# A two-layer diffusion block on one core: layer 0's context tiles part at the query projection, tile 2 goes alone to its first expert choice

## The reference, cut to what matters

```python
# layer 0: pooling mixer and grouped attention side by side; layer 1: windowed attention with sinks
h = rmsnorm(x) * (1 + scale) + shift            # shift, scale, gate: SiLU(c) @ ada_w, per layer and stream
u, q, k, v = split(h @ w_in)                    # layer 0: q and k get an RMSNorm per head
y = concat(pool(u), attention(q, k, v)) @ w_out # a context query sees context keys only
x = x + gate * y
# PEER, per tile of 128 tokens, 8 heads
q  = h2 @ w_q                                   # 1024 x 2048: 256 columns a head
s1, s2 = q[..., :128] @ keys1.T, q[..., 128:] @ keys2.T
# top 16 of s1 and of s2 -> 256 pairs -> top 16 pairs: idx, softmax g
a = gelu(u_tab[idx] . h2)                       # 16 rows of 1024 per token and head, gathered
x = x + gate2 * sum(g * a * v_tab[idx])         # 16 more rows of 1024
```

## Time and profile before

| | |
|---|---|
| runs | 2435.02, 2441.13, 2445.78 us |
| span of the profiled execution | 2436.4 us |
| time of the profiled execution beyond its span | none is given |
| busy | PE 1404.1, DVE 1540.4, POOL 1493.3, ACT 353.7 us |
| moved by DMA | 936.93 MB, 385 GB/s over the span |
| chain that ended last | DMA 35%, POOL 22%, PE 21%, DVE 10%, issue 9% |

### The profile page before, as it was taken

The page is one execution under the profiler, slowest core; times in us unless marked ns, Lnnn a source line. Parts: engine busy times, 40 slices in busy tenths (PEclk is TensorE's granted clock), DMA queues, the critical chain, the costliest instruction groups (busy, mean ns, idle before and its releaser), DMA issues.

```text
span 2436.4 us, 22069 instructions
## 1 busy us (share of the span) xinstructions
PE 1404.1 (58%) x7150; PEld 637.7 (26%) x7150; DVE 1540.4 (63%) x4020; ACT 353.7 (15%) x740; POOL 1493.3 (61%) x1546
## 2 busy tenths in 40 slices
PE   7998863456676574345434446458856555434334
PEld 2456420123323251011001113125623133100000
DVE  1339768878945756767776556412799646777543
ACT  1321210122301011011001002112123011000000
POOL 0005677677676766777777677520477775777772
PEclk9999986677787786677567757678988767566556
DMA  9957999999999999999999999996999999999997
GB/s 346 352 188 287 378 406 408 409 409 409 381 405 409 406 407 407 409 409 409 409 409 409 405 409 409 403 337 239 338 408 400 403 408 406 409 409 409 410 410 305
DMA packets 286802, 936.93 MB, mean 385 GB/s; under 512 B 27729, under 2 KB 28513, under 8 KB 286433
## 3 DMA queue, kind: packets, MB, share of 16 engines
q0 software_dynamic: 221184, 805.40, 83.4%
q1 hardware_dynamic: 65504, 130.12, 14.5%
HBM read 934.36 MB, written 1.05 MB: 384 GB/s over the span
## 4 chain that ended last, share of the span: by engine, by line
DMA 35%; POOL 22%; PE 21%; DVE 10%; issue 9%; ACT 2%; SPq 1%; DVEq 0%; POOLq 0%; ACTq 0%
DMA RING<-in_p_v,IDV 19%; POOL RING L868 15%; DMA RING<-in_p_u,IDX 5%; PE acc L1508 5%; PE wk L1762 5%; DVE RING L949 3%; PE wk L1745 3%; PE wk L1586 3%; POOL WR L868 2%; DMA BC<-in_p_v,IDV 2%; DMA X<-in_p_v,IDV 2%; POOL BC L868 1%; DMA RING<-in_o_w_in 1%; POOL H L868 1%; PE wk L1539 1%
## 5 line engine op out<-in xcount | busy, mean ns | idle before, releaser
L949 DVE SCALAR_TENSOR_TENSOR RING<-RING,acc 128x1024 f32<-128x1024 f32 x576 | 687.6, 1219 | 292.9 <-DMA RING<-in_p_u,IDX 272.8
L1508 PE MATMUL acc<-RING,ST 128*32 128x512 f32 x2020 | 531.5, 914 | 521.4 <-DMA RING<-in_p_v,IDV 463.8
L868 POOL DMA_INDIRECT RING<-in_p_u,IDX x576 | 561.7, 975 | 420.7 <-DVE IDX L1257 193.3
L868 POOL DMA_INDIRECT RING<-in_p_v,IDV x505 | 490.7, 972 | 224.5 <-issue 142.0
L1508 PEld LDWEIGHTS acc<-RING,ST 128*32 128x32 f32 x2020 | 99.7, 144 | 750.4 <-issue 743.4
L1508 PE MATMUL acc<-WR,ST 128*32 128x512 f32 x428 | 160.5, 945 | 65.5 <-DMA BC<-in_p_v,IDV 56.1
L1508 PE MATMUL acc<-X,ST 128*32 128x512 f32 x304 | 124.1, 943 | 104.8 <-DMA RING<-in_p_v,IDV 104.8
L868 POOL DMA_INDIRECT H<-in_p_u,IDX x82 | 78.2, 953 | 126.9 <-DVE IDX L1257 99.2
L949 DVE SCALAR_TENSOR_TENSOR H<-H,acc 128x1024 f32<-128x1024 f32 x82 | 100.0, 1220 | 81.4 <-DMA H<-in_p_u,IDX 80.1
L868 POOL DMA_INDIRECT WR<-in_p_v,IDV x107 | 101.1, 945 | 41.7 <-issue 31.1
L1508 PE MATMUL acc<-BC,ST 128*32 128x512 f32 x156 | 79.3, 947 | 72.4 <-DMA X<-in_p_v,IDV 58.2
(11 more groups left out here) (258 smaller groups left out, 2405.3 us busy)
## 6 DMA issues: line engine op xcount, KB each, us to landing
RING<-in_ada_w SPq DMA_DIRECT2D x25, 1024.0 KB, 14.2
WR<-in_ada_w SPq DMA_DIRECT2D x21, 1024.0 KB, 13.2
WR<-in_p_w_q SPq DMA_DIRECT2D x20, 1024.0 KB, 13.0
RING<-in_p_u,IDX POOLq DMA_INDIRECT x576, 17.6
WR<-in_e_w_in SPq DMA_DIRECT2D x8, 1024.0 KB, 11.7
RING<-in_p_v,IDV POOLq DMA_INDIRECT x505, 18.4
...
```

Source lines behind the costliest of these rows:

```text
L868: pool.indirect_dma_start(out=row_at(row), out_offset=None, in_=tables[kind], in_offset=bass.IndirectOffsetOnAxis(ap=rows, axis=0)).then_i ...
L949: nc.vector.scalar_tensor_tensor(out=row_at(row), in0=row_at(row), scalar=1.0, in1=acc[:, 1, :], op0=ALU.mult, op1=ALU.mult, accum_out=A[: ...
L1508: ins = nc.tensor.matmul(acc[32 * g:32 * g + 32, 0, hf * 512:hf * 512 + 512], ST[:, c % 2, s, :], row_at(rows[g][0])[:, hf * 512:hf * 512 ...
```

## The change

Layer 0's front and its steps 0 to 7 are written anew:
- `("in", 0, 1)` (most of q) is cut into tile 2 and tile 3, on the same kept blocks. Tile 2's q norm stands between them; tile 3's, and its transpose, inside the attention.
- `("ada", 1, 0, 2)` (4 blocks) moves from ahead of the attention to behind `out`; `("ada", 0, 10, 2)` (4 blocks) moves behind the score of head 1; `("ada", 1, 2, 1)` (2 blocks) moves to step 4, `("ada", 1, 3, 1)` from step 4 to 5.
- `out`, `normA`, `normB`, `hT` and `score` of heads 0 and 1 run for tile 2 alone. A score of one tile alone has a new form: tokens stand still and 256 weight columns pass (8 products), the result is turned by two transposes ("T") and multiplied with the keys (2 products); before, weights stood still and each head took 16 products.
- Tile 3's `out` moves to step 0, its norm to steps 1 and 2, its heads 0 and 1 to step 3, on kept blocks. The scores of both tiles move: heads 2 and 3 from ahead of step 0 to step 2, heads 4 and 5 from 0 to 4, heads 6 and 7 from 3 to 5.
- The choice for heads 2 and 3 starts at step 3 instead of 1, later ones by about one step.
- `block_slots` loses its fixed round: each block takes the allowed slot that is idle longest.
- `BC` row 0 is no longer lent to the first `u` gathers, and `H` row 0 to `v` from step 4 instead of 0.
- The ten small loads are issued by ACT's queue instead of SP's.
- Switches `ALONE` and `HEAD_FIRST` go; layer 1 keeps its order, but its scores take the new form.

```diff
-    s += [("in", 0, 1, ctx), ("adaT", 0, 6, 2), ("adaD", 0, 6, 2)]
-    s += [("poolB", CTX, 0), ("poolB", CTX, 1), ("poolB", CTX, 2), ("poolB", CTX, 3)]
-    s += [("rope", 0, t, "q", p) for t in ctx for p in range(2)]
-    s += [("ada", 1, 0, 2), ("adaT", 1, 0, 2), ("adaD", 1, 0, 2)]
-    s += [("tqk", 0, 2, "q"), ("tqk", 0, 3, "q")]
...
+    s += [("in", 0, 1, (2,)), ("rope", 0, 2, "q", 0), ("rope", 0, 2, "q", 1), ("in", 0, 1, (3,)), ("adaT", 0, 6, 2), ("adaD", 0, 6, 2)]
+    s += [("poolB", CTX, g) for g in range(4)]
+    s += [("tqk", 0, 2, "q")]
+    s += att_close(0, CTX, 0, 12, {0: [("rope", 0, 3, "q", 0)], 1: [("rope", 0, 3, "q", 1), ("ada", 0, 8, 2)], 2: [("tqk", 0, 3, "q")],
+                                   3: [("adaT", 0, 8, 2)], 4: [("adaD", 0, 8, 2)], 5: [("bc", 0, CTX, G1)]})
+    s += [("out", 0, (2,), 0), ("outD", 0, (2,), 0), ("out", 0, (2,), 1), ("ada", 1, 0, 2), ("outD", 0, (2,), 1), ("normA", 0, 2, 2), ("normB", 0, 2, 2),
+          ("adaT", 1, 0, 2), ("hT", 0, 2, (2,)), ("adaD", 1, 0, 2)]
+    s += [("score", 0, (2,), (0,)), ("xin", 0, 2), *[("topk", 0, 2, (0,), p) for p in range(3)]]
+    s += [("score", 0, (2,), (1,)), ("ada", 0, 10, 2), ("topk", 0, 2, (1,), 0), ("topk", 0, 2, (1,), 1)]
+    return s + [("adaT", 0, 10, 2), ("adaD", 0, 10, 2)]
...
+    put(f, 0, ("out", 0, (3,), 0), ("outD", 0, (3,), 0), ("out", 0, (3,), 1))
+    next_choices(f, 0, 2, (3, 4, 5, 6, 7))
+    put(f, 1, ("outD", 0, (3,), 1), ("normA", 0, 2, 3))
+    put(f, 2, ("normB", 0, 2, 3), ("hT", 0, 2, (3,)), ("score", 0, ctx, (2, 3)))
+    put(f, 3, ("score", 0, (3,), (0, 1)))
+    put(f, 4, ("score", 0, ctx, (4, 5)))
+    put(f, 4, ("ada", 1, 2, 1), ("adaT", 1, 2, 1), ("adaD", 1, 2, 1))
+    put(f, 5, ("score", 0, ctx, (6, 7)))
+    put(f, 5, ("ada", 1, 3, 1))
...
-    choose(f, 0, 2, (6, 7), (12, 13, 14, 15, 16))
+    choose(f, 0, 2, (6, 7), (13, 14, 15, 16, 17))
...
-EXTRA = [(("bc", 0), "u", 0, 5), (("bc", 1), "u", 0, 5), (("bc", 2), "u", 0, 5), (("h", 0), "v", 0, 22),
+EXTRA = [(("bc", 1), "u", 0, 5), (("bc", 2), "u", 0, 5), (("h", 0), "v", 4, 22),
...
-                sp.dma_start(KR[:, 2 * l, :], t["p_keys1"][l]).then_inc(loaded["keys"], 16)
+                act.dma_start(KR[:, 2 * l, :], t["p_keys1"][l]).then_inc(loaded["keys"], 16)
```

More of the change, by code:

```diff
@@ new lines, in fills1 @@
+    put(f, 0, ("score", 1, first, (4, 5)))
+    put(f, 1, ("score", 1, first, (6, 7)), ("in", 1, 0, second), ("in", 1, 1, second))
+    put(f, 1, ("adaD", 1, 10, 2))
+    put(f, 4, ("rope", 1, 1, "q", 1), ("rope", 1, 1, "q", 2))
+    put(f, 5, ("tqk", 1, 1, "q"))
+    choose(f, 1, 0, (4, 5), (8, 9, 10, 11, 12))
+    att_wide(f, 1, LAT, 5, 8, 16)
+    choose(f, 1, 0, (6, 7), (14, 15, 16, 17, 18))
+    out_blocks(f, 1, second, 17)
+    put(f, 21, ("normA", 1, 2, 1))
+    put(f, 22, ("normB", 1, 2, 1))
@@ L317, in fills1 @@
+    put(f, 23, ("hT", 1, 2, second))
+    for heads, n in zip(((6, 7), (0, 1), (2, 3), (4, 5)), (24, 25, 27, 29)):
+        put(f, n, ("score", 1, second, heads))
+    choose(f, 1, 1, (0, 1), (26, 27, 28, 29, 30))
+    choose(f, 1, 1, (2, 3), (33, 34, 35, 36, 37))
+    choose(f, 1, 1, (4, 5), (40, 41, 42, 43, 44))
+    choose(f, 1, 1, (6, 7), (45, 46, 47, 48, 49))
     put(f, 52, ("normA", 1, 3, 0))
@@ L430, in block_slots @@
 def block_slots():
-    early = next(i for i, name in enumerate(BLOCKS) if name[0] == "score")
     end = AT["ada", 1, 4, 2]
@@ L437, in block_slots @@
     dots = [AT["experts", l, ORDER[l][0], 0, 0] for l in range(DEPTH)]
-    slots, users, idle = [], {}, {s: (-1, s) for s in (*range(WSLOTS), XSLOT)}
+    slots, users, idle = [], {}, {s: (-1, s) for s in range(XSLOT + 1)}
     idle.update({s: (AT["experts_end", 0], s) for s in RSLOTS})
@@ L1350, in _ @@
                     elif (c, tiles[0]) == (2, 0):
-                        for a in range(3):
+                        for a in range(1 - l, 3):
                             act.wait_ge(*emptied(("bc", a), 49 * l))
@@ L1754, in _ @@
                     w = [weights(s + (jh,)) for jh in range(2)]
+                    for h in heads if len(tiles) == 1 else ():
+                        o = begin(s + ("Q", h))
+                        for j in range(KC):
+                            if h == heads[0] and j % 4 == 0:
+                                pe.wait_ge(*evac(tokens + (j // 4,)))
+                            ins = nc.tensor.matmul(o[:, 0:2 * P], HTS[tiles[0] // 2][:, j, tiles[0] % 2 * P:tiles[0] % 2 * P + P],
+                                                   w[j // 4][:, j % 4, h % 2 * 2 * P:(h % 2 + 1) * 2 * P], start=(j == 0), stop=(j == KC - 1))
+                        done(ins)
+                    for h in heads if len(tiles) == 1 else ():
+                        pe.wait_ge(*evac(s + ("Q", h)))
+                        o = begin(s + ("T", h))
+                        for half in range(2):
+                            ins = tr(o[:, half * P:half * P + P], QS[:, h % 2, 0, half * P:half * P + P])
+                        done(ins)
+                    for h in heads if len(tiles) == 1 else ():
+                        pe.wait_ge(*evac(s + ("T", h)))
+                        o = begin(s + ("R", h))
+                        for half in range(2):
+                            ins = nc.tensor.matmul(o[:, half * P:half * P + P], QS[:, h % 2, 1, half * P:half * P + P], KT[:, 2 * l + half, :],
+                                                   start=True, stop=True)
+                        done(ins)
+                    if len(tiles) == 1:
+                        continue
                     for h in heads:
```

219 lines of the change are left out of this document (71 added, 148 removed).

## The result

The changed kernel took 2493.34 us (four runs, 2486.21 to 2494.24), the kernel before, run beside it, 2443.45: 1.0205 of it, 95% interval 1.0184 to 1.0226. The forecast was +26 us on the median and the time is +50, 2.3 us past the upper end of the stated range (2491); the profiled span went from 2436.4 to 2484.4, +48.0. The direction was right, the size half.

A forecast was written before the change was run, and what follows sets the result against it. Gathers were taken as bound by bytes at 409 GB/s, the front as starving the DMA. A 53rd gather 28.6 us later, less 3.2 for bytes, plus 1.1 for layer 1 gave +26: 2441.1 to 2467 us, range 2425 to 2491.

The forecast's parts named there:

- Small loads: Start of the front: with ACT issuing the ten loads, SP's weight blocks start earlier, -4.4 us (bounds 0 and -4.4).
- Query projection: Front, ahead of `out`: split by tile, with tile 2's norm under tile 3's part, -7.2 us (bounds 0 and -11.9).
- `out` to hT: Front, tile 2 alone: from the start of `out` to hT 21.1 us instead of 35.5, -14.4 us.
- hT to IDX: Front, first score and choice: 18.2 us instead of 22.3, -4.1 us (bounds -2 and -5), IDX written at 165.3.
- Step 1: DVE behind the first IDX: tile 3's `out` from 172.8 to 179.8, its norm ready at 199, TensorE waiting from 187.
- Steps 2 and 3: Score of heads 2 and 3 done at 218, tile 3's products end at 229.7; `v` 2 waits until then, DMA idles 30 us.
- Steps 4 to 6: First `v` sums from 237.7, `ada` 1 2 landing at 265.5, DVE waiting until 269, heads 6 and 7 until 290.5, latent hT 307.
- Step 7: POOL's 53rd gather, into H row 3, at 307 instead of 278.43: 28.6 us later, less 3.2 us for bytes moved, 25.4.
- Clock: TensorE after waits of 10 us: slower products, four such gaps up to 6.5 us, left to the range; time then 2473.
- Layer 1: Layer 1's lone-tile scores: a transpose and a copy added ahead of its first choice, +1.1 us (bounds 0 and +4).
- the faster one: Rival, chance 0.16: the early IDX carries through, 53rd gather before about 253, gain 9.5 to 19 us, middle 2427.
- The much slower one: Rival, chance 0.11: POOL stops a third time, row sums of head 1 behind `in` 2 and its blocks, 2490 us.

The follow-up runs named there:

- e1: The kernel before with only the ten small loads issued by ACT's queue: 0.9986 of the kernel before.
- e9: The changed kernel run again, unaltered: 1.0212 of the kernel before.
- e14: The kernel before with heads 4 and 5 scored at step 4 instead of 0, heads 6 and 7 at 5 instead of 3: 1.0141 of the kernel before.
- e18: The same kernel as e14, run again on another chip: 1.0134 of the kernel before.
- e10: The changed kernel with scores of heads 4 to 7 at step 3 and `ada` 1 2 and 1 3 at steps 65 to 68: 1.0162 of the kernel before.

## Why the forecast had the sign and half the size

The mechanism stands: an early IDX, then work and single blocks behind the first gathers, and a later gate at H row 3. What failed is the size of that gate, steps 1 to 7 of the prediction: 307 for a measured 326.4, 19.4 of the 21.5 us that the sum is short. Of the 19.4, 9.8 stand at tile 3's `out` already, where the four blocks of `ada` 0 10 were costed as products alone; most of the rest comes between 275 and 317, where the score of heads 6 and 7 took 18.3 us for 16 and single blocks landed in 8 to 10 us where I had costed less. The gain of 3.2 us for bytes did not come either.

- Small loads, -4.4: **failed as put.** In the changed kernel TensorE waits 9.5 and 4.0 us for rows and keys; its query projection still starts 3.3 us earlier (73.75 for 77.04), while in e1 nothing reached `out` (138.06). Why the changed kernel keeps 3.3 is open. The rule of the Trainium skill ("DMA: Bandwidth & Descriptors", Issuing engines are not separate DMA queues) had the missing half: transfers interleave whoever issues them. The trace agrees, with TensorE waiting 4.6 and 7.4 us longer for them in e1; I had used only its half on issue time.
- Query projection, -7.2: right. From the projection to `out` it is 53.2 us for 60.6, -7.4; `out` of tile 2 starts at 126.9 for 126.0.
- `out` to hT, -14.4: right, 147.8 for 147.1.
- hT to IDX, -4.1: 3.0 us too good, 21.2 for 18.2. The first score took 6.48 instead of 3.6; its second block was issued at 144.54. IDX at 168.8 for 165.3.
- Step 1, tile 3's `out` at 172.8: **the first large miss**, 182.6. `ada` 0 10's fourth block shares a slot with its first and was issued at 170.5, when that was used; TensorE waited 4.76 us for it (the row at 178.23), and I had costed the four as products alone. POOL's wait at 180.47 is the same block.
- Steps 2 and 3: the wait for the norm was there (hT at 210.3 for 200); hT and score took 20.8 for 18 and tile 3's score 8.3 for 7.1; POOL resumed at 243.8 for 229.7.
- Steps 4 to 6: first sum 250.4 for 237.7, `ada` 1 2 at 275.3 for 265.5, heads 6 and 7 from 287.6 for 274.5 and until 305.9 for 290.5, `ada` 1 3 over at 316.8 for 297. The waits were right in kind and place, the landings were not. SP's issues:

```profile
268.48 0.92 SPq L750 DMA_DIRECT2D WR<-in_ada_w  x2
277.28 2.44 SPq L750 DMA_DIRECT2D WR<-in_p_w_q  x2
304.05 1.17 SPq L750 DMA_DIRECT2D WR<-in_ada_w  x2
```

  `ada` 1 2 was issued 14.7 us late and its product began 6.8 us behind the issue, where I had 11.7: by luck it was only 9.8 late. The blocks of heads 6 and 7 took 8 to 10 us, for 5.1 and 2.5, and `ada` 1 3 took 8.8. The products were short too: 16.3 and 18.3 us with the keys, for 15.7 and 16.
- Step 7: 326.4 for 307. These 19.4, and the 3.2 us that I took off for bytes, less layer 1's 1.1, are the 21.5 between 26.5 and 48.0. The bytes at the gate were right, 263 GB/s x 326.4 = 85.8 MB for 85.6, but they bought no time: in the 71.6 us behind it the changed kernel moved 384 GB/s and the one before 406. At 350 us the changed kernel had moved 268 GB/s x 350 = 93.8 MB and the one before 323 x 350 = 113.0 MB, 19.3 MB less (the rates are rounded) or 47 us at 409: all of the 48.
- Clock, "up to 6.5 us", kept out of the sum: mis-sized. The granted clock was 0.83 between the first gather and the 53rd against 0.92, and TensorE 16.7 us longer busy. The Trainium skill ("TensorE: Matmul & The Clock Gate", HAM oscillation) says gaps bring the clock down; the trace agrees: in the window with the wait of 7.84 us it shows 0.80 against 1.00; in that with the 4.71 it is 0.84 in both kernels, and the one before has its wait of 10.07 us there.
- Layer 1, +1.1: not seen. From the 53rd gather to the end both profiled executions take 2158.0 us, and the repeat e9 3.3 more.
- Rivals: the faster one claimed that an early IDX carries through; it fell at the 53rd gather (326, not under 253). The much slower one (2490) had the time nearly right by luck: its stop, for the rows of head 1 behind `in` 2, is not in the trace. The stop at 285.74 is one of the forecast's own (step 5), behind DVE, whose wait for `adaD` 1 2 I had ending at 269 and which ended at 281.1.

What was never in the working is that the scores moved behind the gathers would be nearly as costly without the rest. I had read the cost out of kept blocks and slots; e14 and e18 show 33 to 35 of the 48 us at the gate without any kept block of tile 3. The converse holds too: e10, whose scores of heads 6 and 7 stand at step 3 as in the kernel before, still is 1.6% slower and its gate 28.9 us late, with tile 3's `out`, norm and scores in the same place. The parts do not add (28.9 and 33 to 35 are more than 48.0). That each fills the same TensorE time is argued, not shown. How the 26.1 us of added idle time split between landings and DVE's order, no run tells.
